# Delta rule of a hybrid decoder layer: the first chunk's own output products are made in turn with the second chunk's state update products, in the other rows of TensorE

## What is computed

```python
def _gated_delta_chunk(S, q, k, v, g, beta):
    ...
    u = lax.linalg.triangular_solve(a_mat, rhs, left_side=True, lower=True, unit_diagonal=True)
    qk = jnp.einsum('bhid,bhjd->bhij', q, k) * decay
    o = eg[..., None] * jnp.einsum('bhid,bhde->bhie', q, S) + jnp.einsum('bhij,bhje->bhie', qk, u)
    w_last = jnp.exp(gc[..., -1:] - gc)
    S_new = jnp.exp(gc[..., -1])[..., None, None] * S + jnp.einsum('bhjd,bhj,bhje->bhde', k, w_last, u)
    return S_new, o
```

## Time and profile before

| | |
|---|---|
| median of 3 runs | 3446.47 us (3445.43 to 3449.67) |
| profiled execution, its own time | 3449.35 us |
| its span in the profile | 3447.2 us |
| TensorE busy | 3354.9 us, 97% of the span |
| VectorE busy | 1972.3 us, 57% |
| ScalarE busy | 1477.1 us, 43% |
| GpSimd busy | 390.5 us, 11% |

### The profile page before, as it was taken

One profiled execution on the slowest core, in us unless ns is written; L12 is line 12 of the kernel. 1 busy time (PEld: TensorE's weight loads), 2 busy tenths in 40 slices (PEclk: granted clock), 3 DMA queues, 4 the chain that ended last, 5 costly groups with the idle time before them and its releaser, 6 DMA issues.

```text
span 3447.2 us, 60007 instructions
## 1 busy us (share of the span) xinstructions
PE 3354.9 (97%) x24128; PEld 2970.4 (86%) x24128; DVE 1972.3 (57%) x3757; ACT 1477.1 (43%) x2993; POOL 390.5 (11%) x377
## 2 busy tenths in 40 slices
PE   7989999999999999999999999999999999999998
PEld 6877879999999877889898877789898877789897
DVE  4834435553446744577575844478485754478484
ACT  3322334321233544455354544446363544446362
POOL 2201000142422101000001211000000310000000
PEclk9888899999999999999999999999999999999999
DMA  4101002474663211245463211245454211236353
GB/s 176 62 33 51 27 31 80 147 265 138 251 235 106 71 38 45 85 142 171 137 209 124 76 39 43 80 126 183 125 176 172 80 43 41 69 116 187 122 184 95
DMA packets 143474, 394.82 MB, mean 115 GB/s; under 512 B 18384, under 2 KB 20384, under 8 KB 139728
## 3 DMA queue, kind: packets, MB, share of 16 engines
q1 hardware_dynamic: 143200, 390.98, 34.4%
HBM read 356.24 MB, written 35.69 MB: 114 GB/s over the span
## 4 chain that ended last, share of the span: by engine, by line
PE 72%; issue 10%; ACT 2%; DVE 2%; DMA 0%; POOL 0%; POOLq 0%; DVEq 0%; ACTq 0%
PE bank L878 61%; PE bank L1066 1%; PE bank L1302 1%; PE bank L1293 1%; PE bank L1305 1%; PE bank L1041 1%; PE bank L1237 1%; PE bank L1053 1%; PE bank L1211 1%; PE bank L1139 1%; PE bank L1094 0%; PE bank L1217 0%; ACT junk L1696 0%; DVE Tm L2370 0%; PE bank L1248 0%
## 5 line engine op out<-in xcount | busy, mean ns | idle before, releaser
L609 DVE TENSOR_TENSOR wl<-raw,wh 128x512 fp32r<-128x512 f32 (+1 forms) x795 | 748.5, 949 | 618.6 <-ACT wh L602 615.0
L602 ACT CAST wh<-raw 128x512 fp32r<-128x512 f32 (+1 forms) x795 | 635.9, 808 | 475.9 <-PE bank L878 403.7
L878 PE MATMUL bank<-xnT,wh 128*128 128x512 f32 (+2 forms) x2560 | 744.9, 377 | 11.0 <-DVE d_dT L2167 5.1
L878 PE MATMUL bank<-hnT,wh 128*128 128x256 f32 (+2 forms) x3016 | 580.5, 290 | 3.1 <-ACT V L1772 3.1
L878 PEld LDWEIGHTS bank<-xnT,wh 128*128 128x128 f32 x2560 | 451.9, 195 | 84.6 <-issue 13.5
L878 PEld LDWEIGHTS bank<-hnT,wh 128*128 128x128 f32 x3016 | 473.6, 188 | 8.3 <-ACT V L1772 3.7
L878 PE MATMUL bank<-xnT,wl 128*128 128x512 f32 (+2 forms) x1280 | 470.8, 368 | 0.0
L878 PE MATMUL bank<-hid,wh 128*128 128x512 f32 (+1 forms) x1760 | 467.6, 353 | 0.0
L878 PE MATMUL bank<-hnT,wl 128*128 128x256 f32 (+2 forms) x1508 | 437.2, 290 | 0.0
L878 PE MATMUL bank<-Tm,wh 128*128 128x256 f32 x2016 | 368.7, 282 | 1.2 <-ACT sg L1772 1.2
L878 PEld LDWEIGHTS bank<-hid,wh 128*128 128x128 f32 x1760 | 309.4, 188 | 46.0 <-issue 0.2
(11 more groups left out here) (341 smaller groups left out, 4726.9 us busy)
## 6 DMA issues: line engine op xcount, KB each, us to landing
raw<-in_wstream SPq DMA_DIRECT2D x346, 512.0 KB, 3.5
raw<-wsum SPq DMA_DIRECT2D x252, 256.0 KB, 3.3
raw<-in_wstream SPq DMA_DIRECT2D x189, 256.0 KB, 2.7
ops_in<-in_wstream SPq DMA_DIRECT2D x44, 512.0 KB, 7.5
wsum<-ops_out SPq DMA_DIRECT2D x22, 1024.0 KB, 6.4
xr<-in_x_prompt SPq DMA_DIRECT2D x16, 512.0 KB, 6.9
hT<-in_xT SPq DMA_DIRECT2D x4, 2048.0 KB, 9.2
out_yp_out<-hT SPq DMA_DIRECT2D x16, 512.0 KB, 3.0
```

What stands on the lines that cost most here:

```text
L602: act.copy(hi_cell(n), raw_cell(n)).then_inc(sem("hi_done"), 1)
L609: nc.vector.tensor_tensor(lo_cell(n), raw_cell(n), hi_cell(n).bitcast(F32), ALU.subtract).then_inc(sem("lo_done"), 1)
L878: ins = nc.tensor.matmul(*a, **k)
```

## The change

The own output products of chunk 0 are no longer made behind chunk 0's state update. They wait until chunk 1's state update products and are made in turn with these: own output product of head x (rows 0 to 63, array columns 64 to 127, bank 1), then state update product of head x (rows 64 to 127, all columns, bank 3). The own output products of chunk 1 follow as before. ScalarE's wait and copy of bank 1 move behind the two `beside` calls. `own_o` is a small helper with the same operands as before.

```diff
                         rs = slice(CH * k, CH * (k + 1))
                         ob = (1, 5)[k]
-                        other = slice(CH * (1 - k), CH * (2 - k))
...
                         pe.wait_ge(*made("u_done", F + e + 1))
                         claim(3, "S_done", NH * (F + e + 1))
+                        own_o = lambda j, x: nc.tensor.matmul(
+                            bank[(1, 5)[j]][CH * (1 - j):CH * (2 - j), P * x:P * (x + 1)], QK[CH * j:CH * (j + 1), x, :],
+                            u[CH * j:CH * (j + 1), x, :], start=False, stop=True, skip_group_check=True)
                         for x in range(NH):
+                            if k == 1:
+                                first_o = own_o(0, x)
                             last = nc.tensor.matmul(bank[3][:, P * x:P * (x + 1)], kw[rs, x, :], u[rs, x, :], start=True, stop=True)
                         last.then_inc(sem("dS_ps"), 1)
-                        for x in range(NH):
-                            last = nc.tensor.matmul(bank[ob][other, P * x:P * (x + 1)], QK[rs, x, :], u[rs, x, :],
-                                                    start=False, stop=True, skip_group_check=True)
-                        last.then_inc(sem("o_ps"), 1)
+                        if k == 1:
+                            first_o.then_inc(sem("o_ps"), 1)
+                            for x in range(NH):
+                                last = own_o(1, x)
+                            last.then_inc(sem("o_ps"), 1)
                         beside(t, 15 + 2 * k)
...
-                else:
-                    act.wait_ge(*made("o_ps", F + 2 * t + 1))
-                    act.copy(o_rows[0:CH], bank[1][CH:, :].rearrange("p (h e) -> p h e", h=NH)).then_inc(sem("ob_rd"), 1)
                 beside(t, 15)
                 beside(t, 16)
                 if t != "S":
+                    act.wait_ge(*made("o_ps", F + 2 * t + 1))
+                    act.copy(o_rows[0:CH], bank[1][CH:, :].rearrange("p (h e) -> p h e", h=NH)).then_inc(sem("ob_rd"), 1)
                     act.wait_ge(*made("o_ps", F + 2 * t + 2))
```

## The result

The changed kernel takes 3491.41 us (median of 4 runs, 3488.23 to 3491.76) against 3446.97 us (4 runs): ratio 1.0123, interval 1.011 to 1.0135. The forecast was 3471 us, with a range from 3437 to 3480. The profiled execution took 3491.48 us, 42.1 us more than that of before; its span went from 3447.2 to 3489.3 us.

What follows compares the result with a forecast made beforehand. TensorE was taken to bound the kernel; (2.04 - 0.50) us a tile x 16 tiles = +24.6 us, which takes the median from 3446.47 to 3471 us, range 3437 to 3480.

Steps and rivals of the forecast that it cites:

- What bounds the kernel: Whole kernel: TensorE, busy 97% of the span, under 1 us a tile to spare; its added or removed work reaches the end.
- the first copy's cover: Chunk 0's output copy on ScalarE, 0.58 us, runs while TensorE makes chunk 1's own products; uncovered, at worst 9 us in all.
- Changes of shape are paid, other rows or not: Interleaved part at chunk 1: each tile shape change costs extra although rows differ; likeliest case, 3463 to 3478 us, chance 0.60.
- Term +2.04 a tile: Interleaved part at chunk 1: four pairs of 0.42 and 0.36 us take 3.12 us against 1.08, +2.04 us a tile.
- Gain behind chunk 0: Behind chunk 0's state update: own outputs of 1.02 us removed, partly covering the wait for S; -0.50 us a tile.
- ScalarE and VectorE cost nothing: Output copies and S updates at chunks 0 and 1: order unchanged or nothing late, so no time added.
- TensorE's clock doesn't decide: Clock 0.99 of full speed in group 1, 0.87 in group 0; extra time there costs some 3 us, within the range.
- The rival at 3493 us: Interleaved part at chunk 1: each product's two records also split, every record paying; +2.90 us a tile, +46 us, chance 0.07.
- The overlap rival: Interleaved part at chunk 1: row halves run together despite unequal shapes, nothing added; -8 us, 3438 us, chance 0.26.

Runs made afterwards that it cites:

- e1: The change, but chunk 0's own output products made in turn with chunk 1's own, behind an unbroken state update block; 3449.21 us, 1.0005 of the kernel before.
- e9: e2 with chunk 0's own output products made in turn with chunk 1's own instead of its state updates; 3440.47 us, 0.998 of the kernel before.
- e5: The change with the first gate quarter from behind the interleaved part put in its middle, groups 1 to 3; 3487.91 us, 1.0118 of the kernel before.
- e6: The change with a gate quarter from ahead of the interleaved part put in its middle, 9 tiles of groups 1 to 3; 3476.65 us, 1.0084 of the kernel before.
- e2: The change with each state update product split into two of 64 columns, so all tiles there are 64*64; 3432.64 us, 0.9958 of the kernel before.
- blocks: The change with chunk 0's four own output products as one block ahead of chunk 1's state update block; 3454.40 us, 1.002 of the kernel before.
- pairs: The change with two own output products, then two state update products, and so again; 3463.75 us, 1.0046 of the kernel before.

## Why the prediction was wrong, point by point

- **What bounds the kernel**: right as to TensorE. That TensorE has "well under 1 us" to spare in a tile is a little low: without the wait at the stage's start it is 0.8 us a tile by rows 2 and 1.1 by rows 10. The prediction also saw what would follow if the first copy's cover were gone, 0.58 us a tile ahead of the gate copy; e1 and e9 are decided by that, and e5 by the same gate copy.
- **Changes of shape are paid, other rows or not**: right. Term +2.04 a tile, measured +2.01; 0.42 and 0.36 us a product in both. The range of this case (3463 to 3478) should by its own two terms be 3465 to 3479; nothing hangs on that.
- **Gain behind chunk 0**: sized 0.50, measured 0.39. TensorE starts 0.15 us after the first S is done (VectorE starts at 1235.41 and takes 0.34, L1292 starts at 1235.90) and not 0.06, and its block is not quite dense.
- **ScalarE and VectorE cost nothing**: right for the change. Chunk 0's copy does run under chunk 1's own outputs.
- **The step that failed** is "TensorE's clock doesn't decide", with "some 3 us, which the range takes in". I read the clock only as a price on work that was there already (0.87 in group 0) and never asked whether the new stretch would bring it down. It does: behind eight changes of shape the clock was at 1.2 GHz for 3.4 us of dense gate products, and e6, which only moves a dense quarter into that stretch, is 14.8 us faster. The measured 44.4 us are about 26 of shapes, which the sum had to within 1.3 us, and about 16 to 18 of clock. No rival had it. The rival at 3493 us, records split one by one, is near the time by chance; its part would have been 5.5 us long, and it is 4.11.
- **The overlap rival** (0.26) was refuted where it stood, and true of another kernel: with equal shapes the halves do overlap, and e2 is 0.4% faster. Its case from rows 7 was weaker than it was told: L1248's 16 records have 64 moving columns each, so only L1253's can be compared with 8 records of 128. In the change the weight load of the first state update product starts together with its matmul, at 1240.97, though its rows are not those of the own output product ahead of it.

Open: what exactly brings the clock down. Behind the part the runs show no fall with blocks, one in 12 tiles with pairs, 9 in 12 with eight changes in a row, and none in the tiles with a dense quarter between (12 in e5, 9 in e6). In e2, as well as in e6, TensorE's clock is that of before.

## What to carry to other kernels

In this kernel products in different rows of the array ran together only where their tiles had one shape. So make the shapes equal first, by splitting the wider product into halves of columns, and only then interleave. A sum of busy time for a new pattern on TensorE is incomplete until one has asked what the clock does behind it, and the dense work that follows pays that bill. When a filler is moved or an output made later, read first what it covered on the other engines.

## What the runs showed of the hardware

- One change between 64*64 and 64*128 tiles and back costs 0.34 us with float32 products of 128 columns (0.42 + 0.36 against four records at 0.11), though the tiles lie in different rows. The Trainium skill, "TensorEngine Tiling (Array Packing)", Key Properties, says that a change of the tiling mode drains TensorE. These runs agree in that every change is paid for; that it is a drain they do not show.
- Three 64*64 tiles, one in rows 0 to 63 and two in rows 64 to 127, took three float32 products in the time of one: 24 records in 0.93 us.
- TensorE's granted clock fell from 2.4 to 1.2 GHz right behind a stretch in which the profile shows it 100% busy (4.10 of 4.10 us), and in 9 of 12 tiles at or just ahead of the end of such a stretch; a fall of 3.4 us cost 1.2 us. I had taken a busy TensorE as enough to leave the clock out of the sum.
